# First weight unit loaded by quarters and halves, and later requests for the turned x and x, in a two-block float32 network on one core

## What is computed

```python
def memory_attention(mq, mem, w_kv):
    kv = mem @ w_kv                      # 256 x 2048 times 2048 x 4096: the program's first work
    mk, mv = kv[..., :MEM_WIDTH], kv[..., MEM_WIDTH:]
    ...
def retention_branch(x, positions, w_in, norm_g):
    h = x @ w_in                         # the work after it
    ...
```

## Time and profile before

| what | value |
|---|---|
| median of three runs | 2758.88 us |
| profiled execution: its time, its span | 2757.61 us, 2755.8 us |
| TensorE matmul busy | 2733.2 us (99% of the span) |
| GpSimd busy | 2337.7 us (85%) |
| ScalarE, VectorE busy | 1397.1 us (51%), 1281.1 us (46%) |
| DMA moved | 504.66 MB, mean 183 GB/s |

### The profile page before, as it was taken

How to read it: one execution, slowest core, us unless ns; L and a number is a source line. 1 busy time by engine, 2 the same in 40 slices (tenths; PEclk the granted TensorE clock), 3 DMA queues, 4 the chain that set the end, 5 groups by cost and what they waited for, 6 DMA issues and landing times.

```text
span 2755.8 us, 38662 instructions
## 1 busy us (share of the span) xinstructions
PE 2733.2 (99%) x12660; PEld 2272.9 (82%) x12660; DVE 1281.1 (46%) x2732; ACT 1397.1 (51%) x1873; POOL 2337.7 (85%) x1831
## 2 busy tenths in 40 slices
PE   9999999999999999999999999999999999999998
PEld 7888888888878888888888887888878888888886
DVE  4232234224652675856756465646253323233235
ACT  5544444444454665665665544655454444444444
POOL 8988898888888866877877787888789999999997
PEclk9999999999999999999999999999999999999999
DMA  8655565555565544544544555555555556565553
GB/s 327 200 189 183 185 197 187 183 187 169 178 238 185 184 138 161 168 161 155 175 160 154 163 173 184 168 168 186 178 182 185 195 185 198 191 197 189 198 188 132
DMA packets 283604, 504.66 MB, mean 183 GB/s; under 512 B 17953, under 2 KB 68305, under 8 KB 282449
## 3 DMA queue, kind: packets, MB, share of 16 engines
q1 hardware_dynamic: 274656, 482.08, 53.5%
q10 hardware_dynamic: 8816, 20.86, 2.1%
HBM read 500.75 MB, written 2.12 MB: 182 GB/s over the span
## 4 chain that ended last, share of the span: by engine, by line
POOL 73%; issue 26%; POOLq 1%; PE 0%; DVE 0%; DVEq 0%; ACT 0%
POOL wlo L433 73%; POOLq L431 0%; POOLq L428 0%; DVE x_sb L2623 0%; PE acc L549 0%; POOLq L433 0%; PE acc L551 0%; PE acc L550 0%; POOLq L166 0%; DVE big L2611 0%; DVE kv L1904 0%; DVEq L166 0%; ACT small L1558 0%; DVE small L2618 0%; POOL eps_sb L427 0%
## 5 line engine op out<-in xcount | busy, mean ns | idle before, releaser
L433 POOL TENSOR_TENSOR wlo<-raw,whi 128x512 fp32r<-128x512 f32 x1824 | 2337.2, 1317 | 401.6 <-ACT whi L1102 386.6
L1102 ACT ACTIVATE whi<-raw 128x1024 fp32r<-128x1024 f32 x910 | 957.9, 1059 | 1064.0 <-PE acc L512 1016.6
L510 PE MATMUL acc<-whi,a_lo 128*128 128x512 f32 x2512 | 992.7, 395 | 2.8 <-POOL wlo L433 2.4
L512 PE MATMUL acc<-whi,a_hi 128*128 128x512 f32 x2512 | 978.6, 390 | 0.0
L511 PE MATMUL acc<-wlo,a_hi 128*128 128x512 f32 x2512 | 978.0, 389 | 0.0
L510 PEld LDWEIGHTS acc<-whi,a_lo 128*128 128x128 f32 x2512 | 471.9, 188 | 101.5 <-POOL wlo L433 4.7
L512 PEld LDWEIGHTS acc<-whi,a_hi 128*128 128x128 f32 x2512 | 471.5, 188 | 99.4
L511 PEld LDWEIGHTS acc<-wlo,a_hi 128*128 128x128 f32 x2512 | 472.0, 188 | 96.2 <-issue 1.4
L510 PE MATMUL acc<-whi,b_lo 128*128 128x512 f32 x928 | 365.5, 394 | 0.0
L512 PE MATMUL acc<-whi,b_hi 128*128 128x512 f32 x928 | 361.3, 389 | 0.0
L511 PE MATMUL acc<-wlo,b_hi 128*128 128x512 f32 x928 | 361.2, 389 | 0.0
(11 more groups left out here) (334 smaller groups left out, 2044.2 us busy)
## 6 DMA issues: line engine op xcount, KB each, us to landing
raw<-in_w_in_ret SPq DMA_DIRECT2D x176, 512.0 KB, 4.3
raw<-in_w_in_gdn SPq DMA_DIRECT2D x176, 512.0 KB, 4.3
raw<-in_w_out SPq DMA_DIRECT2D x160, 512.0 KB, 4.5
raw<-in_w_mlp_in SPq DMA_DIRECT2D x128, 512.0 KB, 4.3
raw<-in_w_mlp_out SPq DMA_DIRECT2D x128, 512.0 KB, 4.4
raw<-in_w_in SPq DMA_DIRECT2D x80, 512.0 KB, 4.6
raw<-in_w_mem_kv SPq DMA_DIRECT2D x63, 512.0 KB, 5.1
cb<-log_decays ACTq DMA_DIRECT2D x6, 512.0 KB, 5.2
```

Source lines behind the costliest of these rows:

```text
L433: part = pool.tensor_tensor(wlo[q % 4][:, c], raw_half[:, c], whi[q % 4][:, c].bitcast(f32), ALU.subtract)
L510: pe.matmul(dst, l, w_h, start=start and block == 0, stop=False)
L512: mm = pe.matmul(dst, h, w_h, start=False, stop=stop and block == KB - 1)
L1102: act.activation(whi[q % 4][:, :], raw[j][:, (q % 2) * HALF:(q % 2 + 1) * HALF], ACT.Copy).then_inc(hi_ready, 1)
```

## The change

- SyncE requests step 0's weights as two quarters (`first_quarter`, `first_halves[0]`), the second block of the operand between them and the rest (`next_staged`, before on ScalarE's queue), and every later buffer's second half as two pieces. First and second halves of a buffer have semaphores of their own, so ScalarE waits for the half that it converts.
- ScalarE converts step 0 in two instructions of 512 columns; VectorE rounds the first operand block (`tensor_copy` to `a_hi`), ScalarE only copies it to the bank.
- GpSimd's and TensorE's step 0 wait by quarters; GpSimd's unit 0 stands outside its loop. The matmuls on ones are 14 in place of 20.
- The turned x is requested behind the conversions of unit 1, x (as two requests of 1024 columns) behind those of unit 2; the constants stay behind those of unit 0.

```diff
@@ first_unit (SyncE)
+                for j in range(4):
+                    view = raw[j][:, :].rearrange("p (k c) -> p k c", k=KB)
+                    rows = w[COL * j:COL * (j + 1), 0:COL].rearrange("(k p) c -> p k c", p=P)
+                    if j == 0:
+                        sp.dma_start(view[:, 0, :], rows[:, 0, :]).then_inc(first_quarter, 16)
+                        sp.dma_start(view[:, 1, :], rows[:, 1, :]).then_inc(first_halves[j], 16)
+                    else:
+                        sp.dma_start(view[:, 0:2, :], rows[:, 0:2, :]).then_inc(first_halves[j], 16)
+                    if j == 0:
+                        sp.dma_start(staged_part(1), mem_turned[:, COL:2 * COL]).then_inc(s["next_staged"], 16)
+                    for k in (2, 3):
+                        sp.dma_start(view[:, k, :], rows[:, k, :]).then_inc(raw_loaded[j], 16)
+                    if j < 3:
+                        sp.dma_start(stage(j + 1)[:, :], mem_turned[:, (j + 1) * 1024:(j + 2) * 1024]).then_inc(staged[j + 1], 16)
@@ GpSimd
+            for q in range(8):
+                if q == 0:
+                    pool.wait_ge(s["quarter_ready"], 1)
+                    low(q, quarters[0]).then_inc(s["quarter_low"], 1)
+                pool.wait_ge(hi_ready, q + 1)
+                if q:
+                    low(q, quarters[0])
+                low(q, quarters[1]).then_inc(lo_ready, 1)
+            with pool.Fori(1, UNITS) as m:
...
@@ TensorE
-            for n in range(20):
+            for n in range(14):
                 pe.matmul(acc[1][0][:, 0:P], ones[:, :], ones[:, :], start=True, stop=True)
@@ half (ScalarE)
-                if q % 2 == 0:
+                if isinstance(m, int) and m == U_KV0:
+                    act.wait_ge(*((first_halves[j], 16) if q % 2 == 0 else (raw_loaded[j], 32)))
+                elif q % 2 == 0:
                     act.wait_ge(raw_loaded[j], 32 * m + 32)
@@ ScalarE, the program's start
-            a_part(0, "mem0", 0)
-            act.wait_ge(s["first_half"], 16)
-            act.activation(whi[0][:, :], raw[0][:, 0:HALF], ACT.Copy).then_inc(hi_ready, 1)
-            a_part(1, "mem0", 0)
-            act.wait_ge(raw_loaded[0], 32)
-            act.activation(whi[1][:, :], raw[0][:, HALF:2 * HALF], ACT.Copy).then_inc(hi_ready, 1)
-            for f in range(2, 8):
+            act.wait_ge(first_quarter, 16)
+            act.activation(whi[0][:, 0:COL], raw[0][:, 0:COL], ACT.Copy).then_inc(s["quarter_ready"], 1)
+            act.wait_ge(first_halves[0], 16)
+            act.activation(whi[0][:, COL:HALF], raw[0][:, COL:HALF], ACT.Copy).then_inc(hi_ready, 1)
+            act.wait_ge(a_hi_in, 1)
+            to_bank(0, "mem0")
+            for f in range(1, 8):
                 a_part(f, "mem0", 0)
                 half(U_KV0, f)
...
-            kv_slots(U_KV0, 0, lambda: None, "x0", rotation_and_bound)
+            kv_slots(U_KV0, 0, turned_x_loaded, "x0", x_loaded)
@@ VectorE
+            dve.wait_ge(s["first_staged"], 16)
+            dve.tensor_copy(a_hi[:, 0:COL], staged_part(0)).then_inc(a_hi_in, 1)
+            dve.wait_ge(a_hi_in, 1)
             a_parts("mem0", 0)
```

More of the change, by code:

```diff
@@ L226, in build @@
         raw_loaded = [sem(f"raw_loaded{j}") for j in range(4)]
+        first_halves = [sem(f"first_half{j}") for j in range(4)]
+        first_quarter = sem("first_quarter")
         hi_ready, lo_ready = sem("hi_ready"), sem("lo_ready")
@@ L242, in build @@
             "att_p_turned": "a group's weights of the attention, turned",
-            "first_half": "the first half of the first weights",
             "first_tile": "tile 0 of the last columns of a block",
@@ L247, in build @@
             "first_staged": "the first blocks of the first operand",
+            "quarter_ready": "the high part of the first quarter of the first weights",
+            "quarter_low": "and its low part",
+            "next_staged": "its second blocks",
             "consts_loaded": "masks and frequencies",
@@ L427, in _, with low @@
                 pool.memset(eps_sb[:, n:n + 1], eps).then_inc(s["ones_made"], 1)
-            with pool.Fori(0, UNITS) as m:
+            def low(q, c):
+                at = (q % 2) * HALF
+                return pool.tensor_tensor(wlo[q % 4][:, c], raw[q // 2][:, at + c.start:at + c.stop],
+                                          whi[q % 4][:, c].bitcast(f32), ALU.subtract)
+            quarters = slice(0, COL), slice(COL, HALF)
+            for q in range(8):
[7 more added lines that the diff above has]
+            with pool.Fori(1, UNITS) as m:
                 for q in range(8):
-                    raw_half = raw[q // 2][:, (q % 2) * HALF:(q % 2 + 1) * HALF]
                     pool.wait_ge(hi_ready, 8 * m + q + 1)
-                    for c in (slice(0, COL), slice(COL, HALF)):
-                        part = pool.tensor_tensor(wlo[q % 4][:, c], raw_half[:, c], whi[q % 4][:, c].bitcast(f32), ALU.subtract)
+                    for c in quarters:
+                        part = low(q, c)
                     part.then_inc(lo_ready, 1)
@@ L472, in first_of_all, with product @@
             def first_of_all(m, pair, phase, count):
+                def product(q, k, a, w, start=False, stop=False):
+                    for t in range(TT):
+                        at = (2 * q + k) * SEQ + t * P
+                        mm = pe.matmul(acc[pair][t][:, :], a[:, at:at + P], w[q % 4][:, k * COL:(k + 1) * COL], start=start, stop=stop)
+                    return mm
                 for q in range(8):
-                    pe.wait_ge(hi_ready, 8 * m + q + 1)
                     pe.wait_ge(a_hi_in, 8 * count + q + 1)
[L477 to L487, removed]
+                    if q == 0:
+                        pe.wait_ge(s["quarter_ready"], 1)
+                    else:
+                        pe.wait_ge(hi_ready, 8 * m + q + 1)
+                    product(q, 0, a_hi, whi, q == 0)
+                    if q == 0:
+                        pe.wait_ge(hi_ready, 8 * m + 1)
+                    product(q, 1, a_hi, whi)
+                    low_in(phase, q)
+                    product(q, 0, a_lo, whi)
+                    product(q, 1, a_lo, whi)
+                    if q == 0:
+                        pe.wait_ge(s["quarter_low"], 1)
+                    else:
+                        pe.wait_ge(lo_ready, 8 * m + q + 1)
+                    product(q, 0, a_hi, wlo)
+                    if q == 0:
+                        pe.wait_ge(lo_ready, 8 * m + 1)
+                    product(q, 1, a_hi, wlo, stop=q == 7).then_inc(sub_used, 1)
             def wide_of_new(m, pair, taken, added, between, phase, count):
```

36 lines of the change are left out of this document (17 added, 19 removed).

## The result

The changed kernel takes 2773.36 us (median of five, 2770.91 to 2774.70), beside 2759.95 us for the kernel before (five, 2758.86 to 2760.64). The ratio is 1.0049, with a 95% interval of 1.0039 to 1.0060: slower by 13.4 us, where 2.5 us less were forecast. The profiled execution took 2773.26 us (span 2771.4), against 2757.61.

The account below looks back on a forecast made before the run. TensorE, busy 99% of the span, was taken as the bound, with 2.7 us of waits; 1.4 us (unit 0) plus 1.14 us (unit 1) made 2.5 us, so 2758.88 became 2756.4 us, range 2754.6 to 2758.9.

Parts of the forecast that it names:

- So the 1.14 us of unit 1 go: Unit 1: with x and turned x requested later, weights no longer come late and TensorE's 1.14 us of waits vanish.
- 2 us to spare: Unit 3, step 0: conversion ends at 68.6, low part is there at 71.1, and TensorE comes at 73.1.
- Unit 0's gain: Unit 0: GpSimd begins step 2 1.4 us earlier, so TensorE starts unit 1 at 29.4 instead of 30.81.
- step 1's last quarter: Unit 0: still lands at 7.9, since the same bytes stand ahead of it; converted by 9.0.
- step 2's first half: Unit 0: lands at 10.7 as before and now suffices; converted by 11.75, when GpSimd can begin step 2.
- GpSimd's start on step 2 sets unit 1's start: Units 0 to 1: fourteen low parts of 1.256 us from GpSimd's step 2 set unit 1's start, not TensorE's own start.
- the forecast sum of 2.5 us: Whole kernel: 1.4 us from unit 0 plus 1.14 us from unit 1, giving 2756.4 us.
- the pieces: Rival, unit 0: two more pieces ahead of step 2 delay its weights, unit 0 gains nothing; 2758.0 us, chance 0.10.
- the turned x: Rival, unit 2: the turned x delays it as it did unit 1, moving the 1.14 us gap there; 2757.5 us, chance 0.10.
- the requests: Rival, ScalarE in units 1 and 2: slow requests up to 1.95 us hold it, 2.7 us lost; 2759.1 us, chance 0.06.
- Two of the signs of being wrong: Listed signs: step 2's conversion waiting past 11, gap in units 1 to 3, clock below full after 6 us, x after 98.
- The 2% for "slower": Whole kernel: chance of 0.02 left for a slower result from what had not been seen.

Follow-up runs that it names:

- the version without the two side effects: The changed kernel with the angle steps' operands in PSUM and six 128x8 products on ones behind the fourteen at the start: 2757.72 us, ratio 0.9992.

## Why the prediction was wrong

**The step that failed is "So the 1.14 us of unit 1 go", costed as a pure gain.** I asked what the requests would hold up in their new places, and what the 4 MB would collide with. I did not ask who used the pause of GpSimd that goes with TensorE's gap. The earlier trace rows show the pause (2.00 us ahead of 40.23), and VectorE's first cast lay at its edge. Without the pause the cast waited 30.20 us, and that chain (angles, transposes, bound, the conversions behind them on ScalarE) ended 10.4 us after TensorE was free, with 3.0 us more for the clock.

**The warning was in the trace of before.** VectorE's last three rows shown above took 1.14 to 1.24 us each, the length of a GpSimd instruction, where the changed kernel's same steps take 0.23 to 0.30. I read VectorE's low parts, not its small steps, because VectorE is busy for 46% and TensorE nowhere waited for them. The length of the hold could not be read from that: those steps alternate with GpSimd.

**"2 us to spare" in unit 3 was counted with the requests alone.** ScalarE's two small activations ahead of them on its queue were taken as done on time. They are the path by which VectorE's delay reached TensorE: the conversion that was to end at 68.6 began at 80.23.

**Unit 0's gain was 0.9 us, not 1.4.** The first product came at 5.96 (6.1 forecast). The mis-sized terms are two landings that were taken over from the trace before: step 1's last quarter, put at 7.9, landed at 8.48, and step 2's first half, put at 10.7, at 11.13. ScalarE's conversions waited for both:

```profile
8.51 1.06 ACT L1138 ACTIVATE whi<-raw 128x1024 fp32r<-128x1024 f32 x1 [0.78 <-DMA raw<-in_w_mem_kv]
...
11.15 1.06 ACT L1138 ACTIVATE whi<-raw 128x1024 fp32r<-128x1024 f32 x1 [0.23 <-DMA raw<-in_w_mem_kv]
```

Step 1's low parts ended at 12.18 and step 2's conversion at 12.21, so GpSimd began step 2 at 12.29, not at 11.75:

```profile
12.29 18.83 POOL L440 TENSOR_TENSOR wlo<-raw,whi 128x512 fp32r<-128x512 f32 x15
```

12.29 + 14 x 1.256 = 29.87, and TensorE follows at 29.91. That GpSimd's start on step 2 sets unit 1's start held. Why the two landed later is not shown, and it is one execution: in the five experiments that kept this start, unit 1 begins 0.4 to 1.3 us earlier than before.

**What held.** Unit 1's gap went (the shift grew by 1.2 us there, 1.14 forecast), the requests themselves took 0.91 us for x and held nothing, and the forecast sum of 2.5 us is near what the version without the two side effects gains, 2.4 by the medians. In part that is luck: its trace has 1.1 us from unit 0 (1.4 forecast) and 1.1 from unit 1, and its interval takes in no change. The rivals named the pieces, the turned x and the requests; none had VectorE's small steps or TensorE's instructions in it. Two of the signs of being wrong came, a gap ahead of unit 3 and a clock below full. The 2% for "slower" rested on the cases that I had seen.

**Left open.** The last 2.5 us of the profiled difference lie between 2000 and 2100 us, where the changed kernel's clock was half for a while; eight of the ten experiments' traces have such a stretch there, the kernel before with 14 products among them, and the version without the two waits has none. So it does not follow the change. The record suggests that it goes with the execution: the two experiments without the stretch were traced in the shortest run of their kernel, the trace before is of a run (2757.61) shorter than the five beside which the change was measured, and in the experiments' runs of the kernel before a mean granted clock of 0.999 goes with a median of 2757.5 us (8 runs), 0.997 with 2760.7 (19 runs). What sets it was not tried. Nor was what lets VectorE into a running chain of GpSimd at one time and not at another.

## What to carry to other kernels

Ahead of removing a wait, list what other engines do in the idle time that goes with it; an engine that never pauses can shut another out of what both need, for long though not every time. Small operations on a path that ends at the busy engine are worth a free PSUM bank as operand. Where matmuls that do no work are taken out or put in, look at the whole span for new waits on issue, far behind the edit.

## What the runs showed of the hardware

- A VectorE cast with its operands in SBUF alone that arrived while GpSimd ran back to back was held over 24 GpSimd instructions (30.20 us); with its result in PSUM it took 0.16 us. Behind a pause of 0.19 us the two engines alternated, at 1.2 to 1.3 us a step.
- One small VectorE step with two SBUF inputs, come into a running chain of GpSimd, took 0.47 us in one trace and 9.13 in another.
- TensorE's granted clock was half when it restarted after 10.4 us of idle time, and cost 3.0 us; with products on ones in the gap it stayed full. After the 2 us wait near 1290 us it fell below full in three of six traces.
- Six matmuls fewer at the start gave a wait of 2.08 us at 1290 us, in a kernel that is otherwise the same.
